# A state space stage on one Trainium2 core: inputs and input tables loaded a stage earlier, four tiles scaled there, and the inner products issued ahead of the states

## The chip, the core and the metric

The kernel runs on one NeuronCore of one Trainium2 chip. The metric is the time on the device, in microseconds (us), of one execution. Engines are named as in the profile: PE is TensorE, PEld its weight loads, DVE is VectorE, ACT is ScalarE, POOL is GpSimd, SP is SyncE, which only issues DMAs and waits.

## The reference, cut to what matters

Two blocks follow each other on x of 1024 tokens and 1024 features, all in fp32. The first (a gated recurrent layer, an RWKV layer, their feed-forward parts) is not touched. The second is one hybrid layer:

```python
def hybrid_layer(x, ...):
    h = rms_norm_2(x, pre_g)
    proj = einsum("bld,de->ble", h, w_in)
    conv_in, z_c, u_s, z_s, g_c, g_s = split(proj, IN_OFFSETS)
    ca, cb = split(conv_in, 2)
    cu = ca * sigmoid(cb)
    cu = causal_depthwise_conv_2(cu, conv_w, conv_b)            # 31 taps
    cu = silu(layer_norm(cu, conv_ln_g, conv_ln_b))
    conv_out = einsum("blc,cd->bld", cu * silu(z_c), w_conv_out)
    y = gelu(s5_mimo(u_s, lam_re, lam_im, log_dt, b_re, b_im, c_re, c_im, d))
    y = y * sigmoid(einsum("blc,ce->ble", y, w_glu) + b_glu)
    ssm_out = einsum("blc,cd->bld", y * silu(z_s), w_ssm_out)
    merged = sigmoid(g_c) * conv_out + sigmoid(g_s) * ssm_out
    return x + rms_norm_2(einsum("bld,de->ble", merged, w_out), post_g)

# s5_mimo: 32 groups of 16 channels; per group a complex state of 64 numbers,
#   s_t = Abar s_(t-1) + Bbar u_t ,   y_t = Re(C s_t) + D u_t
```

## The kernel before

The kernel is written engine by engine, with semaphores by name: `tick(name)` adds to one, `after(name, n)` waits for it. It is cut into stages; each ends with its block, in which every engine and SP come to an end before the next block starts. The order of the work on each engine is the order in which the code stands. `H` holds the 1024 x 1024 state as eight tiles of 128 x 1024 (features on partitions).

**The end of the second layer's stage (`HybridIn`).** 48 strips of w_in are multiplied on PE (L303, three fp32r products for each tile, 512 columns at a time). ACT copies each finished strip through its activation to a staging tile and sends it to DRAM: z_c, u, z_s and the gates (`hyd_u` is u). DVE makes the 31 taps, then the layer norm: `ln_c` (subtract the mean, L3493), squares (ACT L3364) and their sum (DVE L3499). PE sums over features with a matrix of 1/1024 (L3354, semaphore `ln_var`), ACT turns it into 1/sqrt (`hy_root`, L3394 and L3396, semaphore `ln_root`), while PE multiplies the last strip. ACT's last store is issued after that strip, and ACT waits for all its stores before the block ends.

**The state space stage (`ssm` in `hybrid`).** u comes back as four tiles k = 0..3 of 128 channels (8 groups of 16). Time is cut into pieces of 8 steps (SC = 8), 128 pieces in all (SN = 128).

- PE `chunks(k)` (8 transposes, L3915), ACT copy to `ssm_uc` (L4008), PE `turned(k)` (8 transposes, L3923), ACT copy to `ssm_ut` (L3996).
- PE `states(k)` (L3935): 16 matmuls of 64 columns with the table `ssm_bt`, into psC; ACT copies them to `ssm_b` (L4002). From k = 2 on that copy waits for `se` of k-2.
- DVE `turns(k)` (L4054 to L4072): rotation with the table `ssm_rot`, two scans along the pieces (L4063, L4065), rotation back into `ssm_e`; semaphore `se`. This is one chain for each k, and the four follow one another. Before each of k = 1..3 stands a copy to `ssm_d` (L4080).
- PE `outputs(k)`: for each of 8 groups one product within the piece, with the table `ssm_toep` on all 128 rows (L3952), then two products for the state that is carried in, with `ssm_cq` on 64 rows (L3954), summed in one place of PSUM. `outputs(1)` goes to psC and so waits for the copy of `states(3)`. ACT copies the result (`sy_c`, L4016), PE `back(k)` transposes it (L3967), ACT applies gelu (L4039), ACT and DVE split y in a high and a low part (L3845, L3749).

Beside this, DVE scales H with gain and 1/sqrt (`tail.normed`, L3836, 6 tiles ahead of the turns, 2 behind), and ACT applies silu (L3841). `ssm_toep` is cleared by POOL (L3906) and then loaded by eight DMAs in rows of 512 bytes and fewer (L3894). SP issues all loads of this stage in one fixed order at its start: u, bt, rot and cq of the first tiles, the eight of toep, then the rest.

**After it** PE multiplies y with w_glu (strips 0 to 3, L303), then with w_conv_out, w_ssm_out and w_out (8 strips each), to the end of the kernel. Weights are loaded by SP (L249), split by ACT in a high part (L260) and by POOL in a low part (L270). The order on PE around the change:

```python
states(2)
outputs(0)
states(3)
back(0)
outputs(1)
back(1)
...
outputs(3)
back(3)
```

## Time and profile before

| | us |
|---|---|
| median of 3 runs (lowest to highest) | 3764.24 (3759.32 to 3765.88) |
| the profiled execution's own time | 3761.57 |
| its span, first to last instruction | 3759.8 |
| PE busy | 3525.5 (94%) |
| DVE busy | 2544.9 (68%) |
| ACT busy | 1510.1 (40%) |
| POOL busy | 1184.3 (31%) |
| mean granted TensorE clock, of 1 | 0.969 |

The table tells how long each engine worked, not what it waited for. For that there are the chain of waits (followed back from the last instruction, printed in order of time), the timeline of each engine (start, busy time, engine, line, operation, count, and in brackets how long the engine was idle before it and what ended that) and the table of stretches, which gives the granted clock of PE too. The clock has two levels, 2.4 GHz (1.00) and 1.2 GHz (0.50).

### The profile page before, as it was taken

Reading aid. Unit: us, or ns where it says so; the run is one execution under the profiler, and the core shown is the slowest. Engines: PE = TensorE matmul, PEld = TensorE weight load, DVE = VectorE, ACT = ScalarE, POOL = GpSimd, SP = SyncE. Lnnn points to the kernel's source line nnn. Section 1 sums busy time; section 2 is a strip of 40 time slices with the busy share of each in tenths; the row PEclk is TensorE's granted clock in tenths of the full one; section 3 lists DMA queues with packets and bytes.
Section 4 is the critical chain, followed back from the end, with each engine's and each line's share of the span. In section 5 each row is a group of like instructions: output and inputs, shape, how many; then the busy total and the mean of one; then the engine's idle time right before and its main releaser. Section 6 shows DMA issues by size and latency. Waiting matters only on the chain. (4 is left out here: it accounts for less than half of the span.)

```text
span 3759.8 us, 55203 instructions
## 1 busy us (share of the span) xinstructions
PE 3525.5 (94%) x23684; PEld 2870.4 (76%) x23684; DVE 2544.9 (68%) x2261; ACT 1510.1 (40%) x1620; POOL 1184.3 (31%) x544
## 2 busy tenths in 40 slices
PE   8999999999999998877788999999998999998996
PEld 6778788888877776677767788878887888876875
DVE  5553776678767866966656676778768888847432
ACT  5464423344443337844454423243444222134322
POOL 1125455445532211244423445455520000000211
PEclk9999999999999999978999999999999999996998
DMA  2112123254312244843323133343312222215322
GB/s 101 51 40 65 61 97 112 90 188 140 104 55 103 84 139 129 266 122 93 94 70 107 64 109 101 104 174 134 118 48 107 73 79 79 79 71 157 122 91 106
DMA packets 215170, 387.76 MB, mean 103 GB/s; under 512 B 16320, under 2 KB 114752, under 8 KB 210944
## 3 DMA queue, kind: packets, MB, share of 16 engines
q1 hardware_dynamic: 177360, 311.88, 25.5%
q10 hardware_dynamic: 37568, 72.36, 5.2%
q8 instruction: 188, 3.08, 0.3%
q14 instruction: 54, 0.44, 0.0%
HBM read 277.76 MB, written 105.91 MB: 102 GB/s over the span
## 5 line engine op out<-in xcount | busy, mean ns | idle before, releaser
L3906 POOL MEMSET ssm_toep<- 128x4096 f32 x1 | 3.5, 3512 | 538.9 <-POOLq L3554 538.9
L3422 DVE SCALAR_TENSOR_TENSOR H<-hy_cu,par,H 128x1024 f32<-128x1024 f32 x120 | 153.4, 1278 | 0.0
L270 POOL TENSOR_TENSOR wlo1C<-fast_raw,whi1C 128x1024 fp32r<-128x1024 f32 (+1 forms) x40 | 112.5, 2812 | 112.5 <-ACT whi1C L260 112.5
L270 POOL TENSOR_TENSOR wlo0B<-fast_raw,whi0B 128x1024 fp32r<-128x1024 f32 (+1 forms) x40 | 112.9, 2822 | 107.7 <-ACT whi0B L260 107.7
L270 POOL TENSOR_TENSOR wlo1A<-fast_raw,whi1A 128x1024 fp32r<-128x1024 f32 (+1 forms) x40 | 111.5, 2786 | 104.0 <-ACT whi1A L260 104.0
L3422 DVE SCALAR_TENSOR_TENSOR hy_odd<-hy_cu,par,hy_odd 128x1024 f32<-128x1024 f32 x112 | 143.1, 1278 | 0.0
L270 POOL TENSOR_TENSOR wlo1B<-fast_raw,whi1B 128x1024 fp32r<-128x1024 f32 (+1 forms) x39 | 107.7, 2763 | 112.2 <-ACT whi1B L260 112.2
L270 POOL TENSOR_TENSOR wlo0A<-fast_raw,whi0A 128x1024 fp32r<-128x1024 f32 (+1 forms) x40 | 109.1, 2727 | 105.0 <-ACT whi0A L260 105.0
L1008 DVE TENSOR_TENSOR fast_xl<-fast_xr,fast_xh 128x2048 fp32r<-128x2048 f32 (+1 forms) x42 | 127.7, 3062 | 21.1 <-ACT fast_xh L849 21.1
L270 POOL TENSOR_TENSOR wlo0C<-fast_raw,whi0C 128x1024 fp32r<-128x1024 f32 (+1 forms) x39 | 108.0, 2768 | 104.3 <-ACT whi0C L260 104.3
L2716 PE MATMUL psA<-sc_XX,sc_NT 64*64 64x32 f32 x2560 | 107.7, 234 | 27.4 <-issue 13.8
L943 DVE TENSOR_TENSOR fast_g<-fast_g,flow_rms 128x1024 f32<-128x1024 f32 x44 | 129.8, 2949 | 1.5
L2949 DVE STREAM_TRANSPOSE sc_XX<-sc_XX 64x512 f32<-64x512 f32 x160 | 112.9, 706 | 20.6 <-POOL sc_XX L2906 15.7
L2722 PE MATMUL psB<-sc_XX,sc_Wt 64*64 64x32 f32 x2560 | 106.6, 233 | 20.0 <-issue 18.2
L2716 PEld LDWEIGHTS psA<-sc_XX,sc_NT 64*64 64x64 f32 x2560 | 96.9, 151 | 34.1 <-issue 18.0
L2722 PEld LDWEIGHTS psB<-sc_XX,sc_Wt 64*64 64x64 f32 x2560 | 97.5, 151 | 21.0 <-issue 19.1
L835 ACT ACTIVATE fast_g<-fast_g 128x1024 f32<-128x1024 f32 x44 | 46.6, 1059 | 129.6 <-DVE fast_g L943 129.6
L2965 DVE TENSOR_TENSOR sc_XX<-psB,sc_XX 128x256 f32<-128x256 f32 x80 | 33.9, 424 | 95.4 <-PE psB L2722 94.8
L270 POOL TENSOR_TENSOR wlo0C<-wraw0A,whi0C 128x1024 fp32r<-128x1024 f32 (+1 forms) x16 | 39.4, 2461 | 169.2 <-ACT whi0C L260 169.2
L270 POOL TENSOR_TENSOR wlo0A<-wraw0A,whi0A 128x1024 fp32r<-128x1024 f32 (+2 forms) x15 | 33.1, 2209 | 175.5 <-ACT whi0A L260 175.4
L2454 DVE SCALAR_TENSOR_TENSOR flow_rms<-flow_rms,hawk_room_b 128x1024 f32<-128x1024 f32 x10 | 12.3, 1225 | 102.7 <-ACT flow_rms L2293 102.7
L849 ACT ACTIVATE fast_xh<-fast_xr 128x2048 fp32r<-128x2048 f32 (+1 forms) x42 | 74.1, 1765 | 12.2 <-DMA fast_xr<-ffn_x 12.2
(1457 smaller groups left out, 11658.6 us busy)
## 6 DMA issues: line engine op xcount, KB each, us to landing
fast_raw<-ffn_in_dram SPq DMA_DIRECT2D x88, 512.0 KB, 3.8
fast_xr<-ffn_x SPq DMA_DIRECT2D x28, 1024.0 KB, 6.0
fast_raw<-ffn_out_dram SPq DMA_DIRECT2D x32, 512.0 KB, 3.8
sc_ops<-rw_arbkv SPq DMA_DIRECT2D x14, 1024.0 KB, 5.9
wraw1A<-hybrid_in_dram SPq DMA_DIRECT2D x24, 512.0 KB, 3.5
wraw1B<-hybrid_in_dram SPq DMA_DIRECT2D x24, 512.0 KB, 3.5
ffn_x<-fast_g ACTq DMA_DIRECT2D x22, 512.0 KB, 3.2
ffn_x<-fast_e ACTq DMA_DIRECT2D x22, 512.0 KB, 2.8
```

The source lines that it names most:

```text
L270: eng.tensor_tensor(self.slot(wlo, n), self.raw[n], self.slot(whi, n).bitcast(fp32), ALU.subtract)\
L835: act.activation(g[:, :, z, :], g[:, :, z, :], ACT.Silu).then_inc(*tick("q_silu"))
L849: act.activation(part(hx, v, i), part(lr, v, i), ACT.Copy).then_inc(*tick("x7_hi"))
L943: dve.tensor_tensor(g[:, :, h, :], g[:, :, h, :], wide(h), ALU.mult).then_inc(*tick("q_g"))
L1008: dve.tensor_tensor(part(lx, v, i), part(lr, v, i), part(hx, v, i).bitcast(fp32), ALU.subtract)\
L2454: dve.scalar_tensor_tensor(out=e, in0=e, scalar=1.0, in1=tz, op0=ALU.add, op1=ALU.mult)\
L2716: mw = pe.matmul(part_of_tile(eight[iw % 2][half(e), m, :], lw, 0), NT[half(1 - e), iw % NTS, m, :], part_of_tile(XX[half(1 - e), cw % 4, ...
L2722: mx = pe.matmul(part_of_tile(eight[2 + ix % 2][half(e), m, :], lx, 1), Wt[lx][half(e), m, :], part_of_tile(XX[half(e), cx % 4, 0, m, :], ...
L2949: dve.transpose(XX[half(1 - e), n % 4, 1, :, :].rearrange("p m t -> p (m t)"), XX[half(e), n % 4, 0, :, :].rearrange("p m t -> p (m t)")). ...
L2965: dve.tensor_tensor(mine, part(eight[2 + k % 2], l, 1), mine, ALU.add).then_inc(*tick("sc_XX"))
L3422: op = dve.scalar_tensor_tensor(out=acc, in0=c[:, j:j + T], scalar=w, in1=acc, op0=ALU.mult, op1=ALU.add)
L3906: pl.memset(toep[:, :, :], 0.0).then_inc(*tick("st_zero"))
```

## The change

- **Early loads.** In the second layer's stage SP issues, behind the last strip's load, the four loads of `ssm_rot` (after `x12_lo`), of `ssm_bt` (after the last tap) and of `ssm_u` (after the stores of u and `ln_var`), and waits for all twelve before the block ends. They lie in places that this stage has done with. All waits for them in the state space stage are gone.
- **Four tiles scaled early.** DVE scales H[0..3] at the end of the second layer's stage, after `ln_root`. In the state space stage it scales 2 ahead of the turns and 2 behind. ACT's silu stays where it was.
- **Inner products ahead.** `outputs(k)` is cut in `within(k)` (the 8 products with `ssm_toep`) and `carried(k)` (the 16 with `ssm_cq`). Only `carried(k)` waits for `se`. `within(k+1)` stands ahead of `back(k)`.
- `ssm_cq` becomes four tiles, without the 16 unused columns in each row: a row of a tile is now loaded in 8 pieces of 512 bytes instead of one of 4608.
- Places in SBUF move. `ssm_cq` 3 lies where wlo2C is, and so POOL makes the low part of strip 2 only when all outputs are done.

```diff
@@ HybridIn.emit, sync
                     W.load(sp, at[-1])
+                    u, bt, rot = self.early
+                    sp.wait_ge(*after("x12_lo", DT))
+                    for k in range(SU):
+                        sp.dma_start(rot[...k...], ROT_[k, :, :]).then_inc(*tick("sr_in", 16))
+                    sp.wait_ge(*after("taps", (TAPS + 1) * DT))
+                    for k in range(SU):
+                        sp.dma_start(bt[...k...], BT_[k, :, :]).then_inc(*tick("sb_in", 16))
...
+                    sp.wait_ge(*after("ln_var", 1))
+                    for k in range(SU):
+                        sp.dma_start(u[:, k, :], U_[k, :, :]).then_inc(*tick("su_in", 16))
+                    sp.wait_ge(*after("sr_in", 16 * SU))
+                    sp.wait_ge(*after("sb_in", 16 * SU))
+                    sp.wait_ge(*after("su_in", 16 * SU))
@@ HybridIn.emit, vector, at its end
+                    dve.wait_ge(*after("ln_root", 1))
+                    for m in range(4):
+                        dve.scalar_tensor_tensor(out=H[:, m, :], in0=H[:, m, :], scalar=pcol("ln_g2", m), in1=self.root,
+                                                 op0=ALU.mult, op1=ALU.mult).then_inc(*tick("ln_n"))
@@ hybrid
                     @block.gpsimd
                     def _(pl):
+                        W.lo(pl, 1)
+                        pl.wait_ge(*after("pe_yc", SU))
                         W.lo(pl, at_wo[-1])
@@ ssm, sync (all of load_u, load_bt, load_rot are gone)
                 load_cq(0)
                 sp.wait_ge(*after("st_zero", 1))
...
-                load_rot(1)
-                load_bt(3)
-                load_cq(1)
-                load_rot(2)
-                load_cq(2)
-                load_rot(3)
-                load_cq(3)
+                for k in range(1, SU):
+                    load_cq(k)
@@ ssm, tensor
-                def outputs(k, groups=range(8)):
-                    pe.wait_ge(*after("se", k + 1))
-                    pe.wait_ge(*after(f"sq_in_{k}", 16))
+                def within(k):
                     if k == 0:
                         pe.wait_ge(*after("st_in", 16 * SC))
                     elif k == 1:
                         pe.wait_ge(*after("sb_b", SU))
                     else:
                         pe.wait_ge(*after("sy_c", 2 * k - 2))
-                    for g in groups:
+                    for g in range(8):
+                        pe.matmul(place(k, g), ut[:, 8 * k + g, :], toep[:, 8 * k + g, :], start=(g < 2), stop=False)
+
+                def carried(k):
+                    pe.wait_ge(*after("se", k + 1))
+                    pe.wait_ge(*after(f"sq_in_{k}", 16))
+                    for g in range(8):
                         q, rows = g // 2, slice(64 * (g % 2), 64 * (g % 2) + 64)
-                        to = ps[3 - k % 2][:, g % 2, q * P:(q + 1) * P]
-                        pe.matmul(to, ut[:, 8 * k + g, :], toep[:, 8 * k + g, :], start=True, stop=False)
                         for z in range(2):
-                            mm = pe.matmul(to, ee[rows, k, z, q, 0:SN], cq[rows, k, z, q, SSM_H:], start=False, stop=(z == 1))
-                    if groups[-1] == 7:
-                        mm.then_inc(*tick("pe_yc"))
+                            mm = pe.matmul(place(k, g), ee[rows, k, z, q, 0:SN], cq[k][rows, z, q, :], start=False, stop=(g >= 6 and z == 1))
+                    mm.then_inc(*tick("pe_yc"))
...
                 states(2)
-                outputs(0)
+                within(0)
+                carried(0)
                 states(3)
+                within(1)
                 back(0)
-                outputs(1)
+                carried(1)
+                within(2)
                 back(1)
-                outputs(2)
+                carried(2)
+                within(3)
                 back(2)
-                outputs(3)
+                carried(3)
                 back(3)
@@ ssm, vector
-                for k in range(6):
+                for k in range(4, 6):
                     tail.normed(dve, k)
```

PE's order at the first two output steps, before: the end of `outputs(0)`, `states(3)`, `back(0)` and the start of `outputs(1)`.

```order
L3952 MATMUL psD<-ssm_toep,ssm_ut 128x128
L3954 MATMUL psD<-ssm_cq,ssm_e 128x128 x2
L3935 MATMUL psC<-ssm_ut,ssm_bt 64x128 x16
L3967 MATMUL psA<-const,ssm_u 128x128 x8
L3952 MATMUL psC<-ssm_toep,ssm_ut 128x128
L3954 MATMUL psC<-ssm_cq,ssm_e 128x128 x2
```

The changed kernel at the same place, from `states(2)` to `within(2)`. L3938 is `states` there, L3954 `within`, L3962 `carried`, L3974 `back`; `ssm_cq_30755` is the table's tile for k = 0.

```order
L3938 MATMUL psC<-ssm_ut,ssm_bt 64x128 x16
L3954 MATMUL psD<-ssm_toep,ssm_ut 128x128 x8
L3962 MATMUL psD<-ssm_cq_30755,ssm_e 128x128 x16
L3938 MATMUL psC<-ssm_ut,ssm_bt 64x128 x16
L3954 MATMUL psC<-ssm_toep,ssm_ut 128x128 x8
L3974 MATMUL psA<-const,ssm_u 128x128 x8
L3962 MATMUL psC<-ssm_cq_30756,ssm_e 128x128 x16
L3954 MATMUL psD<-ssm_toep,ssm_ut 128x128 x8
```

PE now turns from 128-row to 64-row matmuls once for each k, where it did so eight times. `within(0)` has come ahead of the wait for `se`, and `within(k+1)` ahead of the step that waits for the next one.

SP's queue at the turn from the one stage to the other, in the changed kernel (L3577 ends the second layer's block):

```order
L3330 DMA ssm_rot<-ssm_rotd 128x1024 x4
L3333 DMA ssm_bt<-ssm_btd 128x1024 x4
L3339 DMA ssm_u<-hyd_u 128x1024 x4
L3577 UNCONDITIONAL_BRANCH
L3895 UNCONDITIONAL_BRANCH
L3898 DMA ssm_cq_30755<-ssm_cqd 128x8x128
L3904 DMA ssm_toep<-ssm_gdd 16x4096
```

The twelve loads of u, bt and rot stand ahead of the block's end; the eight loads of toep have only one load ahead of them in their own stage.

## Rows read from the trace of the kernel before

**Rows 1.** Table of stretches, state space stage: busy us (records), PEclk, DMA share, GB/s.

```profile
core 0: us, PE busy (x) PEld busy (x) DVE busy (x) ACT busy (x) POOL busy (x), PEclk, DMA share, GB/s
...
3385.25:3389.60 4.35, 0.00 (x0) 0.00 (x0) 4.11 (x4) 0.00 (x0) 3.51 (x1) 0.50 0.77 252
3389.60:3396.60 7.00, 5.84 (x26) 5.11 (x28) 6.87 (x6) 2.21 (x3) 0.00 (x0) 0.50 1.02 414
3396.60:3408.60 12.00, 10.64 (x136) 9.50 (x134) 8.63 (x11) 7.79 (x8) 0.00 (x0) 1.00 1.12 167
...
3410.80:3413.70 2.90, 2.83 (x16) 2.23 (x17) 2.12 (x5) 2.76 (x3) 0.00 (x0) 1.00 0.99 394
3413.70:3427.20 13.50, 13.50 (x66) 10.74 (x64) 12.92 (x18) 6.98 (x8) 0.00 (x0) 0.50 0.53 213
3427.20:3437.30 10.10, 9.68 (x58) 7.42 (x56) 9.72 (x12) 6.47 (x7) 3.22 (x2) 0.99 0.11 28
3437.60:3478.50 40.90, 37.95 (x127) 30.05 (x128) 21.96 (x23) 11.82 (x13) 1.27 (x1) 0.50 0.27 97
```

**Rows 2.** Chain of waits in order of time: start, us, what.

```profile
3385.25 4.35 DMA ssm_u<-hyd_u
...
3423.70 3.64 PE psC L3935 x32
...
3472.73 1.09 ACT ssm_u L4016 x2
...
3473.87 1.97 PE psB L3967 x8
```

**Rows 3.** Timeline of PE, ACT and DVE at the end of the second layer's stage.

```profile
3368.13 1.96 PE L3354 MATMUL psB<-hy_total,const 128*128 128x512 f32 x4 [0.39 <-DVE hy_total L3499]
...
3372.99 1.06 ACT L3396 ACTIVATE hy_root<-hy_root 128x1024 f32<-128x1024 f32 x1
...
3382.08 0.33 ACTq L3387 DMA_DIRECT2D hyd_gs<-hy_stage  x1
...
3385.35 0.09 DVE L4075 MEMSET ssm_e<- 128x32 f32 x1 [17.37 <-PEq L3554]
```

**Rows 4.** Timeline of DVE, state space stage.

```profile
3389.21 7.27 DVE L3836 SCALAR_TENSOR_TENSOR H<-H,par,hy_root 128x1024 f32<-128x1024 f32 x6
...
3399.63 1.42 DVE L4054 TENSOR_TENSOR ssm_tm<-ssm_b,ssm_rot 128x512 f32<-128x512 f32 x2 [3.15 <-ACT ssm_b L4002]
...
3410.85 0.42 DVE L4080 COPY ssm_d<-ssm_decay 128x508 f32<-128x508 f32 x1
3411.95 1.42 DVE L4054 TENSOR_TENSOR ssm_tm<-ssm_b,ssm_rot 128x512 f32<-128x512 f32 x2 [0.68 <-ACT ssm_b L4002]
...
3423.18 0.42 DVE L4080 COPY ssm_d<-ssm_decay 128x508 f32<-128x508 f32 x1
...
3436.77 0.42 DVE L4080 COPY ssm_d<-ssm_decay 128x508 f32<-128x508 f32 x1
...
3442.85 2.28 DVE L4065 TENSOR_TENSOR_SCAN ssm_b<-ssm_d,ssm_tm 128x512 f32<-128x512 f32 x1
...
3448.79 0.69 DVE L4072 TENSOR_TENSOR ssm_e<-ssm_e,ssm_tm 128x512 f32<-128x512 f32 x1
```

**Rows 5.** Timeline of PE and its weight loads: output groups at full and half clock.

```profile
3429.56 0.30 PEld L3952 LDWEIGHTS psC<-ssm_toep,ssm_ut 128*128 128x128 f32 x2
...
3429.98 0.52 PEld L3954 LDWEIGHTS psC<-ssm_cq,ssm_e 64*128 64x128 f32 x4
...
3443.55 0.50 PEld L3952 LDWEIGHTS psD<-ssm_toep,ssm_ut 128*128 128x128 f32 x2 [0.22 <-issue]
...
3444.28 0.93 PEld L3954 LDWEIGHTS psD<-ssm_cq,ssm_e 64*128 64x128 f32 x4 [0.23 <-issue]
```

**Rows 6.** Timeline of SP, and of POOL beside the turns.

```profile
3389.93 17.09 SPq L3894 DMA_DIRECT2D ssm_toep<-ssm_gdd  x8
...
3442.78 1.27 POOL L270 TENSOR_TENSOR wlo2C<-wraw2A,whi2C 128x512 fp32r<-128x512 f32 x1 [7.31 <-ACT whi2C L260]
```

More of the change, by code:

```diff
@@ L3288, in __init__ @@
                 self.W, self.xh, self.xl, self.tail = W, xh, xl, tail
-                self.tmp, self.stage, self.cu, self.odd, self.sg, self.gain, self.total, self.square, self.root = room
+                self.tmp, self.stage, self.cu, self.odd, self.sg, self.gain, self.total, self.square, self.root, self.early = room
                 others = [("u", i) for i in range(SU)] + [("zs", i) for i in range(SU)]
@@ L3326, in _ @@
                     W.load(sp, at[-1])
+                    u, bt, rot = self.early
+                    sp.wait_ge(*after("x12_lo", DT))
+                    for k in range(SU):
+                        sp.dma_start(rot[:, k, :, :, :].rearrange("p z q n -> p (z q n)"), ROT_[k, :, :]).then_inc(*tick("sr_in", 16))
+                    sp.wait_ge(*after("taps", (TAPS + 1) * DT))
+                    for k in range(SU):
+                        sp.dma_start(bt[:, k, :, :, :].rearrange("p z q n -> p (z q n)"), BT_[k, :, :]).then_inc(*tick("sb_in", 16))
+                    for k in range(SU):
+                        j = stored.index(("u", k))
+                        sp.wait_ge(*after(f"hy_out_{j % 4}", 16 * (j // 4 + 1)))
+                    sp.wait_ge(*after("ln_var", 1))
+                    for k in range(SU):
+                        sp.dma_start(u[:, k, :], U_[k, :, :]).then_inc(*tick("su_in", 16))
+                    sp.wait_ge(*after("sr_in", 16 * SU))
+                    sp.wait_ge(*after("sb_in", 16 * SU))
+                    sp.wait_ge(*after("su_in", 16 * SU))
                 @block.tensor
@@ L3690, in glu_gate @@
                             if m == 0:
-                                act.wait_ge(*after("ln_n", DT))
+                                act.wait_ge(*after("ln_n", DT - 4))
                             if m >= 2:
@@ L3839, in silu @@
             def silu(self, act, k):
-                act.wait_ge(*after("ln_n", k + 1))
+                if k >= 4:
+                    act.wait_ge(*after("ln_n", k - 3))
                 act.activation(H[:, k, :], H[:, k, :], ACT.Silu, bias=pcol("ln_b2", k)).then_inc(*tick("ln_act"))
@@ L3852, in scalar, with ssm @@
                 self.high(act, k, y)
[L3854 removed]
+        def ssm(block, at, early, y, tail):
             HS = SC * SSM_H
[L3856 to L3863 removed]
+            u, bt, rot = early
+            b, d0 = at("ssm_b", [P, 2, 2, 4, SN], fp32, 20), at("ssm_d0", [P, 4, SN], fp32, 28)
+            tm = at("ssm_tm", [P, 3, 4, SN], fp32, 30)
+            toep, ut = at("ssm_toep", [P, SSM_G, HS], fp32, 36), at("ssm_ut", [P, SSM_G, SN], fp32, 52)
+            ee = at("ssm_e", [P, SU, 2, 4, SN + 1], fp32, 88)
+            cq = [at(f"ssm_cq{k}", [P, 2, 4, HS], fp32, kib) for k, kib in enumerate((104.125, 108.125, 112.125, 68))]
+            uc = at("ssm_uc", [P, 2, 8, SC, SSM_H], fp32, 136)
             yc = u[:, :, :].rearrange("p k t -> p (k t)").rearrange("p (k i g h) -> p k i g h", k=SU, i=SC, g=8)
@@ L3910, in chunks @@
                 def chunks(k):
-                    pe.wait_ge(*after(f"su_in_{k}", 16))
                     if k >= 1:
@@ L3928, in states @@
                     pe.wait_ge(*after("su_t", k + 1))
-                    pe.wait_ge(*after(f"sb_in_{k}", 16))
                     if k >= 1:
@@ L4054, in two @@
                         ch(dve.tensor_tensor(o, a, p, op))
-                    dve.wait_ge(*after(f"sr_in_{k}", 16))
                     dve.wait_ge(*after("sb_b", k + 1))
```

68 lines of the change are left out of this document (26 added, 42 removed).

## The prediction

> **What bounds the kernel now.** I read the chain of waits first. At 3385.25 us the state space stage starts with a wait of 4.35 us for the first tile of u [rows 2]. From there to the end of `back(3)` at 3473.87 + 1.97 = 3475.84 the chain runs through PE, ACT and DVE, and behind that point it is PE with its strips. So a microsecond gained before 3475.84 is a microsecond of the whole time, as long as the strips behind it find their weights. The table of stretches [rows 1] shows that PE is not simply full: from 3437.6 to 3478.5 it ran at a granted clock of 0.50, and the same from 3413.7 to 3427.2. The timeline of DVE [rows 4] shows the second chain: the four `turns` run from 3399.63 to 3448.79 + 0.69 = 3449.48, nearly without a gap. PE ends 26.4 us after it. The timeline at the end of the stage before [rows 3] shows idle places: DVE was idle for 17.37 us until the new stage began, and ACT's last store was issued at 3382.08.
>
> **The early loads, and the start.** The wait of 4.35 us goes, if all twelve loads land before the old stage ends. The last four, u, are issued when the L3354 matmul is done, 3368.13 + 1.96 = 3370.1. They are 2.1 MB, and large loads moved 414 GB/s in 3389.60:3396.60 [rows 1], so they take 5.1 us; with the 4.35 us of a first landing they are there by 3379.6. The stage lasts until 3385.25 because of ACT's last store, so 5.7 us are to spare. The eight loads of bt and rot come earlier still. I cost them at nothing; if they all were late the price is at most the 4.35 us. Every step to the first rotation on DVE is PE, ACT and PE again behind u, so it moves by 4.35 if the clock rises at the same step as before (rivals): from 3399.63 to 3395.28.
>
> **The four scalings.** DVE's six took 7.27 us [rows 4], 1.21 each, from 3389.21 to 3396.5. With the rotation due at 3395.28 they would be 1.2 us late. Two take 2.4 and end at 3391.6. The four that moved start when `hy_root` is there, 3372.99 + 1.06 = 3374.05 [rows 3], and end at 3378.9, in DVE's idle time. Worth 0 beyond the 4.35, but without them 1.2 of it would be lost.
>
> **The turns.** One takes 11.20 us: 3399.63 to the copy at 3410.85, less its 0.02 of gap. The 0.68 idle ahead of the second [rows 4] is put down to ACT's copy, but that turn needs only the copy of `states(1)`, long done. What it also waits for is rot(1), which SP could issue only behind the eight loads of toep, at 3389.93 + 17.09 = 3407.02 [rows 6]. It goes. The second turn then ends at 3395.28 + 11.2 + 0.46 + 11.2 = 3418.1. The third took 3423.64 to 3436.74, 13.1 us; two of its operations ran long beside POOL, and POOL's two operations stay in that neighbourhood, so I keep 13.1: it ends at 3431.7. The fourth took 12.25 us, 3437.23 to 3449.48, with a scan of 2.28 beside POOL's low part of strip 2 (3442.78, 1.27 us [rows 6]). That one now waits for the last output, so the turn takes 11.2: `se` of k = 3 comes at 3431.7 + 0.5 + 11.2 = 3443.4, against 3449.48. DVE's chain gains 6.1 us: 4.35 + 0.68 + 1.05.
>
> **PE's outputs.** In a group at half clock the weight loads of L3952 take 0.50, then PE's loader is idle 0.23, those of L3954 take 0.93, then it is idle 0.22 [rows 5]; at full clock 0.30 and 0.52, with 0.12 between. Inside a run of one kind there is no such gap. The gaps stand only where PE goes from 128 rows to 64 or back, and of these turns 16 for each k become 2. So at full clock `within` takes 8 x 0.30 = 2.4 us (bound above: 8 x 0.42 = 3.4, the gap kept) and `carried` 8 x 0.52 = 4.2 (above: 8 x 0.64 = 5.1). At half: 4.0 (5.8) and 7.4 (9.2). The rows have no 64-row run that changes from the upper rows to the lower; that is why I keep the upper bounds. In the Trainium skill, "TensorE: Matmul & The Clock Gate", Part 3, weight loads overlap a running matmul only when the row groups differ; by it the gap is a turn's and the change between halves is free, which gives the lower values.
>
> Now the order. `states(2)` ended at 3408.6 [rows 1] and ends at 3404.3. `within(0)` needs toep. Before, toep's eight loads lay behind 4.8 MB of others; now only cq(0) is ahead. POOL clears toep by 3385.25 + 3.51 = 3388.8 [rows 1]. Before, the small pieces moved behind the large loads, in 3396.60:3408.60; if all of these 12 us were theirs, they land by 3388.8 + 1.3 (cq(0)) + 12 = 3402. If they came as late as before, near 3409, `carried(0)` and `states(3)` would still end by 3419. Then `carried(0)` from 3406.5 to 3411 or 3412, `states(3)` 2 us, and a **new wait**: `within(1)` needs psC, whose copy waits for the second turn, 3418.1 + 1.07 = 3419.2. `back(0)`, `carried(1)`, `back(1)` and all ACT work on y are queued behind it; none is late, because at full clock and with the upper bounds `carried(2)` ends at 3419.2 + 2 x (3.4 + 1.1 + 5.1) = 3438.4, and `within(3)` and `back(2)` at 3442.9; with the lower bounds, and `carried(2)` waiting for the third turn, at 3439.4. Both are ahead of the fourth turn. `carried(3)` starts with the fourth turn, 3443.4, and takes 4.2 to 5.1; ACT's copy 1.13; `back(3)` 1.1 to 1.97. The end is 3449.8 to 3451.6, middle 3450.7, against 3475.84: 25.1 us less. The three copies `sy_c` of k = 0 to 2 (1.09 each [rows 2]) no longer stand on PE's path, since `within(k+1)` fills them.
>
> **What else moves.** cq's loads become 512-byte pieces. Toep's 1.18 MB in at most 12 us are 98 GB/s, large loads have 414: 1.6 MB for k = 1..3 take 4 to 16 us behind 3402, the first third at most 5, and that one is needed after 3421. Nothing. POOL's low part of strip 2 comes at about 3449.5 and is needed 11 us later; strip 4's load behind it waits for that, lands some 7 us after, near 3457, and is needed at 3462. SP's loads of z_c behind it wait for work that is later still. Here 5 us of cover are thin, but there.
>
> **Clock at the end.** PE idles 0.5 to 4 us ahead of `carried(3)`. If the clock falls there, `carried(3)` costs 3.2 to 4.1 us more and the first strips start at half as they did before; if not, the strips gain up to 1.3 us. I take 1.1 us of loss. **Sum:** 25.1 less 1.1 = **24 us**. The profiled execution took 3761.57 and would take 3737.6; it stands 2.67 under the median of the runs, so the forecast is **3740.2 us**.
>
> **Rivals.** They differ in PE's clock and in the gaps.
>
> *Half clock from the outputs on, gaps gone.* PE from 3419.2: three `within` at 4.0, three `carried` at 7.4, four `back` at 1.97, 1.1 for the last copy, 43.2 in all: 3462.4, 13.4 us less, 3750.8 us. For it: PE ran at 0.50 for 40.9 us with 37.95 us busy. Against: it then had two idle places in each group, and these are gone. The clock fell after `outputs(0)` had begun behind an idle 2.2 us, and rose after `states(3)`, whose loads and matmuls stand closest. Chance 0.13, mixtures with the forecast included.
>
> *Half clock, gaps kept* (they belong to something else than the change of rows). 17.4 + 27.6 + 7.9 + 1.1 = 54.0 from 3419.2: 3473.2, 2.7 less, 3761.5 us, no change that can be told. Partly full clock gives all between this and the forecast. Chance 0.12, of which I give 0.08 to a gain that is too small to tell and 0.04 to a mixture above that.
>
> *Slower: the clock never rises in this stage.* In the Trainium skill, "TensorE: Matmul & The Clock Gate", Part 4, transposes don't count as busy for the clock. By that rule the start of this stage would stay at half. The rows: PE ran at 0.50 to 3396.6 and at 1.00 from there, and its only work from 3389.6 until 0.3 us before was transposes [rows 1]; here the trace disagrees with the rule. Worked from rows: 8 transposing steps at 1.97, three `states` at 3.64 [rows 2] and a copy's wait of 1.1 from 3385.3 end at 3413.1; then 5.8 + 9.2 + 3.6 + 54.0 with gaps kept: 3485.7, 9.9 us more than now, 3774.1 us. It decides when PE gets less than about 10 us at full clock in the stage; before it had 12.0 + 2.2 + 2.9 + 10.1 = 27. Chance 0.03.
>
> *The early loads hold the old stage open, or strip 4 comes late:* 4 to 7 us of the 24 given back, 3744 to 3747. For it is only how thin the 5 us of cover are; against it the order of the loads. Chance 0.07.
>
> **How the numbers follow.** The forecast keeps 0.64; 0.01 is for a loss not thought of. A measurement of this kernel can tell about 0.2%, 7.5 us. Faster by more: 0.64 + 0.13 + 0.04 + 0.07 = 0.88. Within: 0.08. Slower: 0.03 + 0.01 = 0.04. The range: below, `back(3)` at 3449.8 and the strips' 1.3 us, 27.3 less than the median, 3736.9, and 2 us for how medians of three scatter (the runs shown span 6.6): 3735. Above, the half clock rival, 3750.8, and the better mixtures of the next one: 3756. Left out are the 0.12 of no change and slower and a few hundredths at the edges.
>
> **What would show it.** Right: no DMA wait on PE at the stage's start; first rotation some 10 us after the start (14.4 before); no idle 0.68 ahead of the second turn; the fourth turn's end followed at once by `carried(3)`; rows of L3954 and L3962 at 0.30 and 0.26 for a product at full clock with no idle between them; granted clock near 1.00 from the copy of `states(3)` on. Wrong: a granted clock of 0.50 through the outputs with PE busy to the end (rivals one and two, told apart by the idle 0.22 in each group), PE waiting for toep, or SP's waits ending behind ACT's last store.

## The result, and the profile after

| us | before | the changed kernel |
|---|---|---|
| median (lowest to highest), 4 runs each, same chip | 3761.78 (3758.8 to 3765.88) | 3735.39 (3729.03 to 3738.24) |
| ratio of the times, with its 95% interval | | 0.9925 (0.9902 to 0.9948) |
| the profiled execution's own time | 3761.57 | 3734.24 |
| its span | 3759.8 | 3732.4 |
| mean granted clock | 0.969 | 0.971 |

It is 26.4 us faster. Forecast were 24, and 3740.2 us; 3735.39 lies 0.4 above the lower end of the range. From the page of the changed kernel:

```profile
span 3732.4 us, 55203 instructions
...
PE 3494.6 (94%) x23684; PEld 2851.2 (76%) x23684; DVE 2546.0 (68%) x2261; ACT 1510.0 (40%) x1620; POOL 1186.2 (32%) x544
```

The same instructions, and PE is busy for 30.9 us less (before: 3525.5). So the gain is not idle time of PE that has gone: the 30.9 us are more than the 27.4 by which the span shrank, and PE does the same work in less time.

The table of stretches, changed kernel, over the state space stage (its columns as in [rows 1]):

```profile
core 0: us, PE busy (x) PEld busy (x) DVE busy (x) ACT busy (x) POOL busy (x), PEclk, DMA share, GB/s
3388.20:3402.00 13.80, 12.40 (x107) 11.17 (x108) 8.99 (x10) 6.26 (x7) 3.51 (x1) 0.70 1.02 122
3402.00:3416.00 14.00, 10.65 (x135) 9.57 (x133) 13.41 (x18) 9.70 (x10) 0.00 (x0) 1.00 0.70 154
3416.00:3421.00 5.00, 0.00 (x0) 0.00 (x0) 4.77 (x7) 3.65 (x5) 0.00 (x0) 0.59 0.00 0
3421.00:3424.00 3.00, 1.23 (x5) 1.23 (x6) 2.86 (x5) 2.29 (x2) 0.00 (x0) 0.50 0.01 3
3424.00:3441.00 17.00, 13.96 (x132) 12.89 (x131) 16.35 (x20) 9.98 (x13) 2.95 (x2) 0.91 0.06 16
3441.00:3447.00 6.00, 0.00 (x0) 0.00 (x0) 5.76 (x8) 2.56 (x2) 0.00 (x0) 0.77 0.00 0
3447.00:3453.40 6.40, 5.14 (x42) 4.81 (x43) 6.15 (x6) 1.16 (x3) 1.99 (x1) 0.68 0.81 282
3453.40:3477.00 23.60, 21.96 (x97) 17.91 (x96) 21.76 (x15) 21.43 (x20) 8.38 (x4) 1.00 0.68 249
```

The 40.9 us at 0.50 of [rows 1] are gone. What is left of low clock stands in and behind two stretches in which PE did nothing at all, 3416 to 3421 and 3441 to 3447. DVE is busy in 5.76 of those 6.00 us: it, not PE, is now the engine that sets the time here. PE's timeline, changed kernel (start, busy, engine, line, operation, count, idle before):

```profile
3388.26 1.94 PE L3919 MATMUL psA<-const,ssm_u 128*128 128x128 f32 x8 [4.25 <-PEq L3577]
...
3407.68 2.05 PE L3954 MATMUL psD<-ssm_toep,ssm_ut 128*128 128x128 f32 x16
3409.97 2.16 PE L3962 MATMUL psD<-ssm_cq,ssm_e 64*128 64x128 f32 x32 [0.23 <-DVE ssm_e L4082]
...
3435.39 2.16 PE L3962 MATMUL psD<-ssm_cq,ssm_e 64*128 64x128 f32 x32 [1.51 <-DVE ssm_e L4082]
3437.48 2.05 PE L3954 MATMUL psC<-ssm_toep,ssm_ut 128*128 128x128 f32 x16
3439.36 1.04 PE L3974 MATMUL psA<-const,ssm_u 128*128 128x128 f32 x8
3447.08 3.95 PE L3962 MATMUL psC<-ssm_cq,ssm_e 64*128 64x128 f32 x32 [6.68 <-DVE ssm_e L4082]
3452.20 1.09 PE L3974 MATMUL psB<-const,ssm_u 128*128 128x128 f32 x8 [1.18 <-ACT ssm_u L4027]
...
3476.73 0.70 PE L303 MATMUL psD<-hb_ch,whi2B 128*128 128x512 f32 x2 [1.64 <-POOL wlo2C L270]
```

PE begins with the block (the 4.25 are the change of blocks, not a load), `within(0)` waits for nothing, and `within` takes 2.05 and `carried` 2.16 at full clock. The last `carried` waited 6.68 us for DVE and then ran at half clock. DVE's timeline, changed kernel:

```profile
3377.07 4.88 DVE L3518 SCALAR_TENSOR_TENSOR H<-H,par,hy_root 128x1024 f32<-128x1024 f32 x4 [6.10 <-ACT hy_root L3412]
...
3388.79 3.22 DVE L4086 COPY ssm_d<-ssm_decay 128x512 f32<-128x512 f32 x1
...
3392.17 2.48 DVE L3862 SCALAR_TENSOR_TENSOR H<-H,par,hy_root 128x1024 f32<-128x1024 f32 x2
3398.72 1.42 DVE L4065 TENSOR_TENSOR ssm_tm<-ssm_b,ssm_rot 128x512 f32<-128x512 f32 x2 [4.06 <-ACT ssm_b L4013]
...
3410.41 1.42 DVE L4065 TENSOR_TENSOR ssm_tm<-ssm_b,ssm_rot 128x512 f32<-128x512 f32 x2
...
3430.43 1.78 DVE L4065 TENSOR_TENSOR ssm_e<-ssm_e,ssm_tm 128x512 f32<-128x512 f32 x1
3432.24 1.64 DVE L4065 TENSOR_TENSOR ssm_e<-ssm_b,ssm_rot 128x512 f32<-128x512 f32 x1
...
3446.33 0.69 DVE L4082 TENSOR_TENSOR ssm_e<-ssm_e,ssm_tm 128x512 f32<-128x512 f32 x1
```

The gap of 0.68 ahead of the second turn [rows 4] is gone; the four turns are one chain from 3398.72 to 3447.02. The two long operations of the third turn stand beside POOL's two.

**Where the 27.4 us between the two spans are.** The stage starts when POOL begins to clear `ssm_toep`: at 3385.2 before, at 3388.2 here. That start moves by itself: in the kernels below it lies between 3374.2 and 3392.9, from what comes before this stage, and most of the scatter of whole times is this. So I count from that start, and call the time from it to the end of the span *start to end*: 374.6 before, 344.2 now.

| us after the start | before | changed | difference |
|---|---|---|---|
| first rotation on DVE | 14.38 | 10.50 | 3.9 less |
| fourth turn ends | 64.2 | 58.8 | 5.4 less |
| `back(3)` ends | 90.59 | 65.07 | 25.5 less |
| first strip of w_conv_out | 115.10 | 88.51 | 26.6 less |
| from there to the end | 259.5 | 255.7 | 3.8 less |
| start to end | 374.6 | 344.2 | 30.4 less |

3.0 of the 30.4 are lost again in the comparison of the two spans, by the later start. The 3.8 behind the stage nobody had forecast. The busy time in the groups of instructions shows it. The products of one strip of the kernel before, between 3488 and 3590 (busy us, mean ns of one, idle before):

```profile
L303 PE MATMUL psC<-hb_ch,whi2B 128*128 128x512 f32 x16 | 5.0, 394 | 0.0
...
L303 PE MATMUL psC<-hb_ch,whi2C 128*128 128x512 f32 x16 | 5.0, 394 | 0.0
```

and of the changed kernel:

```profile
L303 PE MATMUL psC<-hb_ch,whi2B 128*128 128x512 f32 x16 | 4.9, 389 | 0.0
```

Each of the strips' products is 5 to 6 ns shorter. From the starts of successive strips of 48 products: 3533.76 to 3544.90 before is 11.14 us, 3520.36 to 3531.24 now is 10.88. The 3.8 are the sum of two things. From the first conv strip to the start of the kernel's last strip it is 217.63 us before and 212.66 now, 5.0 less. From there to the end it is 41.82 before and 43.01 now, 1.2 more: the four matmuls with `hy_root` for the last norm (L3682, now L3706) take 1.96 us before and 3.52 now, behind 3.47 us of idle time in both.

### The profile page after: what moved, and what is told of

The parts are those of the page before. It is cut to its first block and busy times, and to the rows that moved or that the text cites. A ratio compares the mean times of both kernels' runs of the same rounds, so it can differ in the third digit from the quotient of the medians.

```text
span 3732.4 us, 55203 instructions
## 1 busy us (share of the span) xinstructions
PE 3494.6 (94%) x23684; PEld 2851.2 (76%) x23684; DVE 2546.0 (68%) x2261; ACT 1510.0 (40%) x1620; POOL 1186.2 (32%) x544
## 5 line engine op out<-in xcount | busy, mean ns | idle before, releaser
L1008 DVE TENSOR_TENSOR fast_xl<-fast_xr,fast_xh 128x2048 fp32r<-128x2048 f32 (+1 forms) x42 | 127.7, 3062 | 21.1 <-ACT fast_xh L849 21.1
L2722 PEld LDWEIGHTS psB<-sc_XX,sc_Wt 64*64 64x64 f32 x2560 | 98.9, 153 | 24.4 <-issue 22.4
L2454 DVE SCALAR_TENSOR_TENSOR flow_rms<-flow_rms,hawk_room_b 128x1024 f32<-128x1024 f32 x10 | 12.3, 1226 | 103.5 <-ACT flow_rms L2293 103.5
```

The source lines that it names most:

```text
L1008: dve.tensor_tensor(part(lx, v, i), part(lr, v, i), part(hx, v, i).bitcast(fp32), ALU.subtract)\
L2722: mx = pe.matmul(part_of_tile(eight[2 + ix % 2][half(e), m, :], lx, 1), Wt[lx][half(e), m, :], part_of_tile(XX[half(e), cx % 4, 0, m, :], ...
```

## The experiments

The first question was which part of the change carries the gain, the second what a `carried` costs, the third where the strips' pace comes from, the last what sets the time now. They ran in three sets, each on one chip beside the kernel before: b_batch, a_grouped, a_notahead and a_ring128 beside 3759.76 us (median of 22 runs, 3746.19 to 3768.33), b_again, a_halves, a_six and a_poolwait beside one run of 3770.45, the last four beside 3761.26 (11 runs, 3748.67 to 3773.26).

| kernel | time, us (ratio, 95%) | fourth turn ends | `back(3)` ends | first conv strip | rest | start to end |
|---|---|---|---|---|---|---|
| before | 3761.57 | 64.2 | 90.59 | 115.10 | 259.5 | 374.6 |
| b_again | 3764.19 | 63.7 | 90.46 | 114.96 | 259.2 | 374.2 |
| b_batch | 3743.68 (0.9967, 0.9950 to 0.9983) | 64.9 | 72.79 | 96.32 | 261.2 | 357.5 |
| a_grouped | 3740.33 (0.9957, 0.9941 to 0.9974) | 58.1 | 72.15 | 95.54 | 256.1 | 351.6 |
| a_notahead | 3729.69 (0.9930, 0.9903 to 0.9956) | 57.9 | 65.99 | 89.37 | 256.1 | 345.4 |
| a_halves | 3729.64 | 58.1 | 67.00 | 91.41 | 255.8 | 347.2 |
| a_ring128 | 3734.64 (0.9933, 0.9914 to 0.9952) | 57.9 | 63.85 | 87.33 | 259.7 | 347.0 |
| a_six | 3732.40 | 59.3 | 66.46 | 90.82 | 255.8 | 346.7 |
| a_poolwait | 3735.34 | 56.7 | 63.87 | 88.26 | 255.8 | 344.1 |
| changed | 3735.39 (0.9925, 0.9902 to 0.9948) | 58.8 | 65.07 | 88.51 | 255.7 | 344.2 |
| a_again | 3733.80 (0.9923, 0.9902 to 0.9943) | 58.2 | 64.48 | 87.88 | 255.8 | 343.6 |
| a_tables | 3735.49 | 57.4 | 64.54 | 88.95 | 255.4 | 344.4 |
| a_busy | 3737.35 | 58.2 | 62.69 | 88.94 | 257.2 | 346.2 |
| a_both | 3736.00 (0.9931, 0.9913 to 0.9948) | 56.8 | 61.32 | 87.32 | 257.6 | 344.9 |

Times with a ratio are medians of 4 to 10 runs, the others one execution. The places are those of the profiled execution, counted from the stage's start. Since the start alone moves by up to 19 us, the last column is the one to compare. Two executions of one kernel differ in it by 0.4 (before, b_again) and 0.6 (changed, a_again), which is how far I trust it. That is one pair for each of two kernels; for the others there is one profiled execution.

**b_again**, the kernel before without an edit. 

> The kernel before, unchanged, profiled once more. Disputed is whether its slow outputs (granted clock 0.50 from 3437.6 to 3478.5) belong to the kernel or to how this one execution fell. Theory: the clock's steps fall differently from execution to execution and the stage's length (start to the end of back(3), 90.6 us in the first trace) moves by 5 us or more. Rival: it is within 1 us of 90.6.

It came out as 374.2 with `back(3)` at 90.46. The half clock in the outputs is no accident of one execution.

**b_batch**: before, with the products of one k together.

```diff
-for g in groups:
-    pe.matmul(to, ut[...], toep[...], start=True, stop=False)
-    for z in range(2):
-        pe.matmul(to, ee[rows, ...], cq[rows, ...], ...)
+for g in groups:
+    pe.matmul(place(g), ut[...], toep[...], start=(g < 2), stop=False)
+for g in groups:
+    for z in range(2):
+        pe.matmul(place(g), ee[rows, ...], cq[rows, ...], ...)
```

> The kernel before, with one edit: in outputs(k) the 8 products with ssm_toep stand ahead of the 16 with ssm_cq, at the same place in PE's order and behind the same waits. Theory 1 (the turning between 128-row and 64-row products was the cost, and 64-row products of the two halves run together): outputs(k) takes 2.05 + 2.16 = 4.2 us at full clock, as in the changed kernel, PE is no longer behind DVE, and back(3) ends 7 to 11 us after the fourth turn (64.2 us after the stage's start) instead of 26.4: 15 to 19 us less than before, 0.4 to 0.5%. Theory 2 (the order, the products ahead of the wait, made the gain): within 2 us of before.

PE's timeline, b_batch, the last group:

```profile
3448.16 3.45 PE L3952 MATMUL psC<-ssm_toep,ssm_ut 128*128 128x128 f32 x16 [3.24 <-DVE ssm_e L4074]
3451.54 2.16 PE L3956 MATMUL psC<-ssm_cq,ssm_e 64*128 64x128 f32 x32
3454.87 1.09 PE L3969 MATMUL psB<-const,ssm_u 128*128 128x128 f32 x8 [1.18 <-ACT ssm_u L4018]
```

Theory 1 held. This edit alone brings `back(3)` 17.8 us forward (the time falls by 16.1), and PE then waits for DVE ahead of the last group: 7.9 us lie between the fourth turn's end and `back(3)`'s, against 26.4 before. So the order of the products within one k is the largest part. It leaves DVE's chain where it was, as it must (64.9).

**a_grouped**: the changed kernel with each k's products in the old order, behind `se`.

```diff
-within(0)
-carried(0)
-states(3)
-within(1)
-back(0)
...
+outputs(0)
+states(3)
+back(0)
+outputs(1)
...
```

> The changed kernel, with outputs(k) as it was: group by group, all of it behind the wait for se, in the old order. Early loads and early scaling stay. Theory 1: PE is again the bound of the outputs stage, at 1.06 or 1.87 us a group by the clock; the fourth turn ends 59 us after the stage's start as in the changed kernel, but back(3) some 20 us or more behind it; 5 to 10 us less than before (the strips' faster pace of about 4 us counted in). Theory 2 (the loads made the gain): 20 us or more less than before.

The table of stretches, a_grouped, over its outputs:

```profile
3409.00:3425.00 16.00, 16.00 (x68) 12.63 (x69) 15.32 (x21) 8.44 (x9) 0.00 (x0) 0.50 0.00 2
3425.00:3459.00 34.00, 30.28 (x191) 23.79 (x188) 28.88 (x32) 16.29 (x18) 5.49 (x3) 1.00 0.22 78
```

and the start of its last group but one on PE, in the timeline of a_grouped:

```profile
3454.19 0.49 PE L3957 MATMUL psC<-ssm_toep,ssm_ut 128*128 128x128 f32 x2
3454.61 0.71 PE L3959 MATMUL psC<-ssm_cq,ssm_e 64*128 64x128 f32 x4
3455.25 0.49 PE L3957 MATMUL psC<-ssm_toep,ssm_ut 128*128 128x128 f32 x2
```

Theory 1 has PE as the bound, which it is, but `back(3)` ends 14.1 us behind the fourth turn and not 20 or more, and the time falls by 19.4 us, not by 5 to 10. That is near the 20 or more of theory 2 (23.0 from start to end). With the old order of the products the gain at `back(3)` is 18.4 all the same, though DVE's chain gives only 6.1 of it: the other 12.3 are clock. In this kernel it rose to 1.00 at 3425 and stayed there through all later outputs; in the kernel before it was 0.50 from 3437.6 on [rows 1]. The group costs 1.06 us here (3454.19 to 3455.25), 8.5 for a k; the same group costs the kernel before 1.06 at full clock and 1.87 at half. Why the clock stays up here was not tried; what is left of the change in this kernel are the early loads, the early scaling, the new tiles of `ssm_cq` and the moved places. It is also one execution: its eight timed ones reach from 3734.76 to 3752.07 us, and the last of these has a granted clock of 0.966 against 0.971 to 0.974 in the other seven, so the clock may not come back up each time. The two halves of the change, 17.8 and 18.4, together give 25.5: they do not add. In a_grouped PE still sets the time after 3425, 14.1 us behind DVE, and it is only full clock that it gained. With the new order PE waits for DVE, in b_batch 3.24 us and in the changed kernel 6.68 us ahead of its last part, and from there DVE's chain and the last k are all that is left.

**a_notahead**: the new order within a k, but both parts behind `se` of their k.

```diff
+pe.wait_ge(*after("se", 2))
 within(1)
-back(0)
 carried(1)
-within(2)
 back(1)
...
```

> The changed kernel, batched as it is, but within(k) waits for the same turn as carried(k) and back(k-1) stands ahead of it. Prices what standing ahead is worth. Theory: only the last within stands on the path, 2.05 us at full and 3.8 at half clock: 2 to 4 us more than the changed kernel. Rival (standing ahead fills PE and keeps the clock up, or down): 6 us or more, or less than 1.

345.4 against 344.2 and 343.6: to issue the inner products ahead of the states, which the change is named for, is worth 1 to 2 us of the 30, less than the 2 to 4 of the theory. `within` is short (2.05 us at full clock), and only that of the last k stands on the path: it takes 2.99 us here. Of these 1.14 are given back by the clock: `carried(3)` takes 3.95 us in the changed kernel, after 6.68 us of idle time, and 2.81 here, where PE waited 2.59 us ahead of `within(3)`.

**a_halves**: `carried` takes the even groups (rows 0 to 63) first, then the odd ones (rows 64 to 127).

```diff
-for g in range(8):
+for g in (0, 2, 4, 6, 1, 3, 5, 7):
```

> The changed kernel, but carried(k) takes the even groups first (all on rows 0 to 63) and then the odd ones (rows 64 to 127), instead of alternating. Same products, same places. Theory: carried takes 2.16 us for 32 records at full clock because matmuls of the two halves of the rows run at the same time; without alternation it takes 32 x 0.13 = 4.2 us at full and 7.5 at half clock, and only the last one is on the path: 2 to 4 us more to back(3). Rival (it is fast because nothing of 128 rows stands between): 2.2 us as now.

PE's timeline, a_halves:

```profile
3401.79 3.50 PE L3962 MATMUL psD<-ssm_cq,ssm_e 64*128 64x128 f32 x32 [0.23 <-DVE ssm_e L4082]
```

3.50 us for the same 32 records at the same full clock, against 2.16 where the halves alternate. The starts of the single records in the trace show why: in the changed kernel nearly all come in pairs, 3 to 14 ns apart, one pair every 110 ns or so; here they come one by one, 111 or 112 ns apart, but for three pairs where the even groups give way to the odd ones. So neighbours on different halves of the rows run at the same time. In the Trainium skill, "TensorE: Matmul & The Clock Gate", Part 3, matmuls whose tiles lie in different row groups run concurrently; the 2.16 against 3.50 agree. The theory had 4.2 us here, and the rival, 2.2, fell. `back(3)` ends 1.9 us later than in the changed kernel, 2.5 later than in a_again. From start to end it is 3.0 more (347.2 against 344.2), of which 0.9 is `back(3)`, at half clock in this execution.

**a_ring128**: the changed kernel, with the weights of slots A and B, and three tiles beside them, 128 bytes further up; slot C stays on whole KiB.

```diff
-"wlo2A": 136, "wlo2B": 140,
-"wraw2A": 144, "wraw2B": 148, "whi2A": 152, "whi2B": 156
+"wlo2A": 136.125, "wlo2B": 140.125,
+"wraw2A": 144.125, "wraw2B": 148.125, "whi2A": 152.125, "whi2B": 156.125
```

> The changed kernel, with the places of the weight strips A and B (raw, high and low part) of the last stage 128 bytes further, as they all lay before; strip C's stay on a multiple of 4 KiB. Disputed is why a strip of 48 products takes 10.88 us after the change and 11.15 before. If the 128 bytes of the weights do it, strips of slots A and B take 11.15 and those of C 10.88, some 3 us in all; if it is the place of something else, all stay at 10.88.

The groups of instructions, a_ring128, slot B and slot C between 3488 and 3590:

```profile
L303 PE MATMUL psC<-hb_ch,whi2B 128*128 128x512 f32 x16 | 5.0, 395 | 0.0
...
L303 PE MATMUL psC<-hb_ch,whi2C 128*128 128x512 f32 x16 | 4.9, 390 | 0.0
```

In one kernel, with one program, the strips of the moved slots take the old 11.15 us and those of slot C, left in place, 10.92. From the first conv strip to the start of the last it is 216.06 us, 3.4 more than in the changed kernel: two of three slots give two thirds of the 5.0. So the faster pace comes from where the weights lie, and not from the clock or the order. That the rest comes out at 259.7, as before the change, has 0.6 of chance in it: the part behind the last strip's start took 43.61 here. One thing is left open. In the kernel before only the low part of slot C was 128 bytes off (158.125), its high part lay at 0, and yet its strips took 11.15 us and the products with `whi2C` 394 ns, as shown above. So what counts is not just the address of the one operand that a product reads; which places together make the slower pace was not tried.

**a_six**: all six scalings in the new stage, as before the change. 

> The changed kernel without the early scaling: DVE scales six tiles ahead of the turns, as before. Theory: DVE ends them 8.4 + 2.9 = some 11.3 us after the stage's start, the first turn starts there instead of at 9.7 to 10.5, and all turns and back(3) move by 0.8 to 1.6 us. Rival: none, the copy of states(0) comes later anyway.

The first rotation comes 11.14 us after the start, against 9.90 in a_again: 1.2 us, as forecast. The fourth turn ends 1.1 later than there. Start to end is 3.1 more; 0.9 of it is `back(3)`, which fell to half clock in this execution (1.97 for 1.09), and 0.9 lie between `back(3)` and the first strip of w_conv_out. In those 0.9 the first strips ran at half clock too (1.20 us for the first two products, 0.72 in a_again). So the four scalings are worth 1.1 us, and up to 3 with what follows behind them; that part I can't tell from chance with one execution.

**a_poolwait**: POOL's two low parts (and ACT's high part behind them) wait for the fourth turn.

```diff
+pl.wait_ge(*after("se", SU))
 W.lo(pl, 1)
...
-if k == 1:
-    self.W.hi(act, 2)
 self.high(act, k, y)
+if k == 3:
+    self.W.hi(act, 2)
```

> The changed kernel, with POOL's low parts of strips 0 and 1 held until the fourth turn is done, and ACT's high part of strip 2 behind y of k = 3. Theory: two operations of the third turn no longer take 1.7 us instead of 0.69 beside POOL, the third turn shrinks from 13.2 to 11.2, and the fourth turn and back(3) come 2 us earlier; the strips find their weights in time. Rival: a new wait of PE for the low parts of strips 0 and 1, or for strip 4, gives it back.

From the end of the second turn to that of the third it is now 11.7 us instead of 13.7 (in a_again 13.7 too), so its two long operations were POOL's doing. In the Trainium skill, "SBUF — State Buffer", the rules for kernel authors, when a DVE operation has two SBUF inputs and a GpSimd one reads SBUF, the second to issue is blocked until the first is done; the 2.0 us agree. The copy of 3.22 us at 3388.79, beside POOL's clearing of `ssm_toep`, against 0.42 for the later copies (508 columns instead of 512), looks like the same, but it has one input and no run took the clearing away. But start to end is 344.1. Of the 2.1 us at the fourth turn 1.2 reach `back(3)`, since that now ran at half clock too, 0.25 the first conv strip, and nothing the end. The second loss is clock as well: from `back(3)` to the first conv strip it is 24.4 us, 23.4 in the changed kernel, because the first three pairs of products ran at half. The wait for the weights is no longer than there (1.45 us, 1.64). PE's timeline, a_poolwait:

```profile
3451.34 1.97 PE L3975 MATMUL psB<-const,ssm_u 128*128 128x128 f32 x8 [1.18 <-ACT ssm_u L4028]
3477.70 0.70 PE L303 MATMUL psD<-hb_ch,whi2B 128*128 128x512 f32 x2 [1.45 <-POOL wlo2C L270]
```

and POOL's, a_poolwait:

```profile
3475.11 2.38 POOL L270 TENSOR_TENSOR wlo2C<-wraw2B,whi2C 128x1024 fp32r<-128x1024 f32 x1 [5.47 <-ACT whi2C L260]
```

**a_again, a_tables, a_busy, a_both.** The last set asks whether the two costs that are left on the path, three copies between DVE's turns and PE's fall of clock, can be had. The edits:

```diff
+for k in range(SU):                        # ahead of the first turn, four tiles
+    ch(dve.tensor_copy(ds[k][:, :, :], decay8[:, 4 * k:4 * k + 4]...))
-    if k > 0:
-        ch(dve.tensor_copy(d0[:, :, 1:], decay8[...]...))
```

```diff
 back(2)
+spare(24)      # 24 matmuls of 128x128 into a place that nobody reads (20 in a_both)
 carried(3)
```

> The changed kernel without an edit, beside the two below on the same chip. If the stage is steady from execution to execution, the time from its start (GpSimd's memset of toep) to the end of the span comes out at 344.2 us within 1, as in the changed kernel's first profile, with 0.5 granted in PE's idle time ahead of the last `carried` and carried(3) at 3.9 us. If the clock's state there is a matter of chance, carried(3) may take 2.2 and the stage be 1 to 2 us shorter.

> The three copies of the decay table that stand between DVE's turns (0.42 to 0.43 us each, 0.46 with the gap) are made ahead of the first turn, in three places that are free. Theory (after the change DVE's four turns are the path, PE waits for each): the fourth turn ends 1.4 us earlier after the start, back(3) too, and start to end is 342.8 instead of 344.2. Rival (PE and the clock still set the time): the fourth turn is earlier, back(3) less than 0.5 earlier, 343.8 or more.

> 24 matmuls of 128x128 into a place that nobody reads stand between back(2) and carried(3), in PE's 6.7 us of idle time (24 x 0.26 = 6.2 us). Theory (the idle time ahead of carried(3) is what brings the granted clock down): the clock stays at 1.00, carried(3) takes 2.2 us instead of 3.95 and back(3) 1.1; back(3) ends 1.8 us earlier after the start, 342.4 from start to end. Rival 1 (the clock falls whatever PE does there): carried(3) still 3.9, 344.2. Rival 2 (they hold carried(3) up): it starts later than the end of the fourth turn, up to 346.

> Tables made ahead and 20 matmuls in the idle time. If each is worth what its theory says and they add: 344.2 - 1.4 - 1.8 = 341.0 from start to end, some 3.2 us less than the changed kernel in the same rounds. If only the tables help, 342.8; if neither, 344.2. Differences under about 4 us between whole kernels may drown in how the stages before scatter.

PE's timeline, a_busy (each spare product leaves two records):

```profile
3440.84 5.52 PE L3958 MATMUL psB<-ssm_toep,ssm_ut 128*128 128x128 f32 x48
3447.69 2.16 PE L3966 MATMUL psC<-ssm_cq,ssm_e 64*128 64x128 f32 x32 [1.32 <-DVE ssm_e L4087]
3451.02 1.09 PE L3978 MATMUL psB<-const,ssm_u 128*128 128x128 f32 x8 [1.18 <-ACT ssm_u L4032]
...
3478.36 0.70 PE L303 MATMUL psD<-hb_ch,whi2B 128*128 128x512 f32 x2 [3.88 <-POOL wlo2C L270]
```

With work in PE's idle time the clock stays at 1.00, `carried(3)` takes 2.16 instead of 3.95, and `back(3)` ends 1.8 us earlier than in a_again: the idle time is what brought the clock down. `carried(3)` took 3.94 or 3.95 us in the five executions with 5.1 to 6.7 us of idle time there (the changed kernel, a_again, a_six, a_poolwait, a_tables) and 3.64 in a_ring128; it took 2.16 in both with the spare products. In a_tables the fourth turn ends 1.4 earlier than in the changed kernel, whose first rotation came at the same 10.5, but `back(3)` gains 0.5, because it fell to half clock (1.97), and the first strips after it lose 1.0 more in the same way (`back(3)` to the first conv strip 24.4 us, 23.4 in the changed kernel). In a_both the two add: `back(3)` at 61.32, 3.2 us earlier than in a_again, as forecast. None of it reaches the end: 344.4, 346.2 and 344.9 against 343.6, and in time 3736.0 against 3733.8 (the intervals lie over one another). PE's timeline, a_both, shows where it is lost:

```profile
3452.81 1.09 PE L3979 MATMUL psB<-const,ssm_u 128*128 128x128 f32 x8 [1.18 <-ACT ssm_u L4033]
...
3479.90 1.19 PE L303 MATMUL psD<-hb_ch,whi2B 128*128 128x512 f32 x2 [3.64 <-POOL wlo2C L270]
```

The first strips of w_conv_out wait for the low part of their weights: 0.92 us in the kernel before, 1.57 in a_again, 3.88 in a_busy and 3.64 here. After the last of these they started at half clock (1.19 for two products, 0.70 at full). In a_busy the clock fell one pair of products later. This second fall costs another 1.7 and 2.7 us: from the first conv strip to the start of the last it is 214.3 us in a_busy and 215.4 in a_both, 212.7 in the changed kernel and in a_again. So once the idle time ahead of `carried(3)` is filled, what stands on the path is the flow of the weights. In POOL's timeline, a_both:

```profile
3464.82 4.30 POOL L270 TENSOR_TENSOR wlo2A<-wraw2B,whi2A 128x512 fp32r<-128x512 f32 x1 [11.67 <-ACT whi2A L260]
3469.10 2.40 POOL L270 TENSOR_TENSOR wlo2B<-wraw2A,whi2B 128x1024 fp32r<-128x1024 f32 x1
3477.32 2.36 POOL L270 TENSOR_TENSOR wlo2C<-wraw2B,whi2C 128x1024 fp32r<-128x1024 f32 x1 [5.82 <-ACT whi2C L260]
```

The raw place B is free for the next load only when the first of these is done, SP issues that load at 3469.16, and ACT makes the high part at 3476.21, behind another copy that itself waited 2.43 us for DVE. Which of the two, the load or DVE's work, would hold it if the other went was not tried. No version beat the changed kernel by more than the scatter (a_notahead's 3729.69 is from another chip; its ratio, 0.9930, is not below the changed kernel's 0.9925).

## Why the prediction was right, and where it was not

- **What failed.** The sum was 25.1 us for `back(3)` less 1.1 behind it. Measured from start to end are 25.5 for `back(3)` and 4.9 more behind it, so nearly all of the 6.4 us by which the size is off lie in the part after `back(3)`. The sum had "I take 1.1 us of loss" there and no term for the pace of the strips, which it left at nothing without a reason. The runs showed a gain of 1.1 us up to the first conv strip and of 3.8 from there on, where weights on whole KiB make the strips faster. The step of the mechanism that failed is the price of `carried`, below: half of what was forecast, hidden by a fall of the clock.
- **The bound and the start** held. No load is waited for, the stage before did not end later (ACT's last store is issued 3.1 us ahead of the stage, as in [rows 3]), and of the 4.35 us 3.9 came: 10.50 instead of the forecast 10.0, because `states(0)` took 2.69 us, partly at half clock. In a_again it was 9.90. The rival of late loads fell.
- **The turns** held to 0.1 us. The forecast has them end 21.2, 32.9, 46.5 and 58.2 us after the start (3385.25); a_again has 21.1, 32.8, 46.5 and 58.2. The changed kernel's own profile has 58.8, by the later first rotation. That POOL made the long scan in the fourth turn and that the third turn would keep its length (13.6 from end to end with the copy forecast, 13.7 measured) are borne out. The 0.68 are gone, which fits rot(1) as their cause; no run moved that load alone.
- **The end of `back(3)`** was forecast at 65.45 (3450.7), and came at 65.07. But this hit has two misses in it. The step that failed is "at full clock `carried` 8 x 0.52 = 4.2 (above 5.1)": it takes 2.16. I had read the 0.52 of [rows 5] as the price of four records on one half of the rows, and argued only about the gap; that neighbours on different halves run together was not in the sum. The other is the clock: I set PE's idle time ahead of `carried(3)` at 0.5 to 4 us; with `carried` twice as fast it was 6.7, and ahead of `within(1)` 8.75. So the clock did fall, and `carried(3)` took 3.95. That it is near the 4.2 of the sum is luck. At full clock `back(3)` would have ended at 62.7 (a_busy).
- **The clock in the outputs** came back as forecast, and the rivals of half clock, 3750.8 and 3761.5, fell. But my argument against them, that PE's two idle places in each group are gone, was not the reason: in a_grouped they are all there, 0.42 and 0.64 us to the next as before, and from 3425 on the clock stayed at 1.00. So this hit is in part luck. What decides whether it rises was not settled. That it never rises fell at once: 0.70 in the first 13.8 us, 1.00 from 3402.
- **The 1.1 us of loss in the first strips** did not come. They started at full clock, and between `back(3)` and the first conv strip 1.1 us were gained where 1.1 were to be lost: some 1.4 by the clock of the first six pairs of products and 0.5 by the strips' pace, less 0.7 by the longer wait for weights.
- **The strips after that** are the largest miss: the forecast has no term for them, and they took 3.8 us less, 5.0 from weights that came to lie on whole KiB less 1.2 of clock at the last norm. The diff showed the addresses (150.125 to 136), and I read them as a matter of room alone.
- **The cover of the weights** was 5 us for strip 4, "thin, but there". The rival of a late strip 4 fell, but the next one's weights are later still, and I had not looked at them: PE already waited 0.92 us for them before the change, and 1.64 now (3476.73). That costs 0.7 here, and the same wait with the fall of the clock behind it swallows the gain of a_busy and a_both.
- **The sum**: 24 forecast; in start to end 30.4, made of 25.5 for `back(3)` (25.1 forecast), 1.1 and 3.8. The stage's start was 3.0 us later in this execution, so the spans differ by 27.4 and the medians by 26.4. The path was right; the size was 6.4 us short from start to end, and 3.0 of scatter hid half of that in the times.

## What to carry to other kernels

Price a run of matmuls with few rows by whether neighbours lie on different row groups: a run that alternates can cost 2.16 us where the same work in another order costs 3.50. When PE's share of the path shrinks, ask at once what its new idle time does to its clock, and which of the slower flows (here the low parts of the weights) becomes the next bound: four edits brought the fourth turn or `back(3)` forward, and the gain was lost to half clock in the first products (a_poolwait, a_tables) or in the wait for weights and the clock behind it (a_busy, a_both). And where a change moves tiles, look at the addresses of what TensorE reads later; to tell such small steps apart, count from a place inside the kernel, not from its start.

## What was not expected of the hardware

- Matmuls on 64 rows that alternate between the two halves start in pairs, 3 to 14 ns apart. 32 records of `carried` take 2.16 us at full clock with the halves of the rows alternating and 3.50 without; in groups mixed with 128-row products, 8 x 0.64 = 5.1.
- Weights 128 bytes off a whole KiB make a strip of 48 products 11.15 us instead of 10.88 to 10.92 (394 and 395 ns against 389 and 390 in the groups), at a granted clock of 1.00. It was 11.15 too where only the low part was off. Other offsets were not tried.
- The granted clock fell in idle stretches of 6.7 and 8.75 us, and it also stays down in busy ones: in a_grouped PE was busy for all of 16.00 us at 0.50, and then at 1.00 in the same kind of work. What made it rise there stays open.
